# Table loads of ScalarE written out in the kernel, with Ln and Exp from one table set, in a two-layer streaming encoder

## The reference

```python
def trunk_layer(h, p_l, past_k, past_v, ...):
    mix, k, v, v_a = token_mixers(rmsnorm(h, g_mix), past_k, past_v, ...)
    h = h + mix
    h = h + peer(rmsnorm(h, g_ffn), w_peer_q, sub_keys, u_tab, v_tab)
    gate = jax.nn.sigmoid(rmsnorm(h, g_ple) @ w_ple_gate + b_ple_gate)
    h = h + (p_l @ w_ple) * gate
```

## Time and profile before

| | |
|---|---|
| timed runs, median of 3 (lowest, highest) | 3350.75 us (3350.59, 3355.32) |
| span of the profiled execution | 3616.5 us |
| ACT busy / TABLE_LOADs | 786.7 us / 313 |
| PE, DVE, POOL busy | 67%, 65%, 59% of the span |
| bytes moved, mean rate | 1277 MB, 353 GB/s |

### The profile page before, as it was taken

How to read it: one execution, slowest core, us unless ns; L and a number is a source line. 1 busy time by engine, 2 the same in 40 slices (tenths; PEclk the granted TensorE clock), 3 DMA queues, 4 the chain that set the end, 5 groups by cost and what they waited for, 6 DMA issues and landing times.

```text
span 3616.5 us, 28348 instructions
## 1 busy us (share of the span) xinstructions
PE 2438.9 (67%) x8364; PEld 999.6 (28%) x8364; DVE 2348.9 (65%) x5973; ACT 786.7 (22%) x1403; POOL 2133.1 (59%) x2201
## 2 busy tenths in 40 slices
PE   7547748989855467878554588878965455756546
PEld 4313313443411123334111124334331112211111
DVE  1576596557688876565786766555678776654552
ACT  4104112553100022231000131544200111200012
POOL 0265565556666666666666666555666666666661
PEclk9778869988866679989766799987977767887778
DMA  6599999989989999999999999998999999999993
GB/s 234 211 387 380 357 359 350 336 302 347 376 333 354 353 383 412 414 382 399 360 358 350 363 358 403 362 342 299 398 386 338 366 361 361 412 389 371 365 377 131
DMA packets 330209, 1277.02 MB, mean 353 GB/s; under 512 B 37380, under 2 KB 38404, under 8 KB 322760
## 3 DMA queue, kind: packets, MB, share of 16 engines
q0 software_dynamic: 313344, 1140.99, 83.2%
q1 hardware_dynamic: 16712, 134.21, 9.3%
HBM read 1267.45 MB, written 6.82 MB: 352 GB/s over the span
## 4 chain that ended last, share of the span: by engine, by line
PE 30%; DVE 28%; issue 15%; another core or an unknown queue 9%; POOL 7%; DMA 6%; ACT 5%; DVEq 0%; POOLq 0%; ACTq 0%; SPq 0%
DVE urows L1313 11%; PE experts L1615 9%; PE bank L1585 9%; DMA vrows<-in_peer_v,idx_v 4%; POOL urows L902 4%; POOL vrows L902 4%; PE bank L1595 3%; PE att_out L1585 2%; DVE work L1198 2%; DMA urows<-in_peer_u,idx 1%; DVE part L1274 1%; DVE work L1264 1%; DVE diag L1350 1%; DVE work L1268 1%
## 5 line engine op out<-in xcount | busy, mean ns | idle before, releaser
L1615 PE MATMUL experts<-vrows,diag 128*64 128x512 f32 (+1 forms) x3896 | 1220.7, 765 | 824.2 <-DVE diag L1350 329.3
L1313 DVE CUSTOM_DVE_ANT_0 urows<-urows,query 128x1024 f32<-128x1024 f32 x1088 | 1307.7, 1212 | 302.4 <-DMA urows<-in_peer_u,idx 202.8
L902 POOL DMA_INDIRECT urows<-in_peer_u,idx x1024 | 1005.6, 982 | 547.4 <-issue 289.9
L902 POOL DMA_INDIRECT vrows<-in_peer_v,idx_v x910 | 883.9, 971 | 719.5 <-PE experts L1615 347.1
L1615 PEld LDWEIGHTS experts<-vrows,diag 128*64 128x64 f32 (+1 forms) x3896 | 305.8, 165 | 1577.4 <-issue 1197.9
L1585 PE MATMUL bank<-weights,xT 128*128 128x512 f32 (+1 forms) x1008 | 469.7, 618 | 27.2 <-issue 20.7
L1585 PEld LDWEIGHTS bank<-weights,xT 128*128 128x128 f32 (+1 forms) x1008 | 175.8, 181 | 306.0 <-issue 295.8
L1595 PE MATMUL bank<-xT,weights 128*128 128x288 f32 (+2 forms) x688 | 152.2, 379 | 33.6 <-issue 23.4
L958 ACT ACTIVATE work<-bank 128x256 f32<-128x256 f32 (+2 forms) x67 | 29.2, 437 | 642.5 <-PE bank L1809 199.6
L902 POOL DMA_INDIRECT vrows<-in_peer_v,idx x114 | 114.6, 1005 | 75.7 <-PE experts L1615 32.4
L1361 DVE SCALAR_TENSOR_TENSOR h<-vrows,plain,h 128x1024 f32<-128x1024 f32 x114 | 146.3, 1284 | 0.0
(11 more groups left out here) (212 smaller groups left out, 2556.2 us busy)
## 6 DMA issues: line engine op xcount, KB each, us to landing
weights<-in_w_in SPq DMA_DIRECT2D x25, 2048.0 KB
weights<-in_w_out SPq DMA_DIRECT2D x10, 2048.0 KB
weights<-in_w_peer_q SPq DMA_DIRECT2D x10, 2048.0 KB
urows<-in_peer_u,idx POOLq DMA_INDIRECT x1024
weights<-in_w_ple_gate SPq DMA_DIRECT2D x8, 2048.0 KB
vrows<-in_peer_v,idx_v POOLq DMA_INDIRECT x910
weights<-in_w_ple SPq DMA_DIRECT2D x4, 1024.0 KB
weights<-in_sub_keysT SPq DMA_DIRECT2D x5, 512.0 KB
```

The lines of the kernel that those rows point to most:

```text
L902: pool.indirect_dma_start(out=rows[:, where, :], out_offset=None, in_=table, in_offset=bass.IndirectOffsetOnAxis(ap=index, axis=0))\
L1313: dve.tensor_tensor_reduce(row, row, query[:, :], 1.0, 0.0, ALU.mult, ALU.add, hid[:, j % 2, k:k + 1]).then_inc(dotted.sem, 1)
L1615: last = pe.matmul(experts[c][HALF * x:HALF * x + wide, :], diag[:, (4 * j + q) % ND, k % QUARTER + x, 0:wide], vrows[:, (n + x) % NV, 512 ...
```

## The change

ScalarE's stream asks for its sets itself. A function names the set of each stage, and behind a stage that uses one, the set of the next stage that uses a different one is asked for.

```diff
+LOG_EXP, GELU, SIGMOID = "natural_log_exp_and_others", "gelu_and_others", "sigmoid_and_others"
+
+
+def table_of(s):
+
+    k = s[0]
+    if k in ("ua", "va") or (k == "peer" and s[2] == 0 and 0 < s[1] <= ITEM_COUNT):
+        return GELU
+    if k == "gate":
+        return SIGMOID
+    if k in ("squares", "vaQ", "attQ", "mixQ", "attZ", "samZ", "attE", "samX") or (k == "choice" and s[4] == 0):
+        return LOG_EXP
+    return None
...
+            table_uses = [x for x in SCHEDULE if table_of(x)]
+
+            def next_table(s):
+
+                n = table_uses.index(s) + 1
+                if n < len(table_uses) and table_of(table_uses[n]) != table_of(s):
+                    act.preload_act_table_set(table_of(table_uses[n]))
...
+            act.preload_act_table_set(table_of(table_uses[0]))
             act.wait_ge(const_made, 1)
             for s in SCHEDULE:
...
+                if table_of(s):
+                    next_table(s)
```

## The result

The changed kernel takes **3321.55 us** (median of 4 runs, 3316.86 to 3329.72) against 3352.67 us of the kernel before, timed beside it: a ratio of 0.990, with a 95% interval of 0.9883 to 0.9916, or 31 us less. The forecast was 3309.5 us, 41.3 us less, with a range of 3268 to 3344. Direction and order of size came out; two of the three terms did not have the size that they were given, and their errors partly cancel.

What follows compares the result with a forecast made beforehand. The prediction took transfers to set the pace in most of the kernel, with ScalarE's table loads on the path at the ends and in attention. 7.7 + 5.2 + 28.4 = 41.3 us off 3350.75 gave 3309.5 us, range 3268 to 3344.

Steps and rivals of the forecast that it cites:

- The price of a load: Anywhere on the path: one table load removed from ScalarE lets the next instruction start 1.29 us earlier.
- First tile: Before any gather: six loads on the path, 1.29 us each, bring the first gather forward by 7.7 us.
- The step on the weights: First tile: the 2 MB weight unit lands at about 11 us, barely hidden before TensorE's first product at 11.35.
- Last tile: After the last gather: four loads on the path, at 1.29 us each, save 5.2 us.
- The middle: From 133 to 3547 us: 22 of 42 removed loads on the chain count, all in the attention stretches, 28.4 us.
- the room in the attention stretches: Two attention stretches at 310 and 322 GB/s: transfers could speed up to 361 GB/s, leaving room for 25 and 23 us.
- The loads elsewhere: Middle outside the attention stretches: 20 loads on the chain (25.8 us), counted at nothing because DMA is at 0.94 or above.
- The moved loads: Loads that stay but move, some passing over ScalarE's copies: taken as 0, from 15 us lost to 19 us gained.
- the slower rival: Moved loads delay copies others wait for, 29.9 us in full, and the middle gains nothing: 3368 us, chance 0.08.
- Only the ends: Rival: only first and last tile gain, 12.9 us, as the middle waits for transfers: 3338 us, chance 0.20.
- The whole chain: Rival: all 54.2 us of the middle's chain count besides the ends, 67.1 us in all: 3284 us, chance 0.16.
- the drain: Rival: each table switch costs twice its load, as a hidden drain goes too: 3268 or 3265 us, chance 0.01.

Runs made afterwards that it cites:

- half gathers: Kernel before and changed kernel, each with gathers of 512 floats per token instead of 1024: 3221.83 us with the old loads, 3174.62 us with the change.
- the kernel with the middle alone: Against the kernel before, only the stages between the first and the last gather changed (175 loads): 3337.21 us, ratio 0.9942.
- the second profile: The kernel before, unchanged, profiled once more: span 3350.4 us, timed 3355.81 us, ratio 0.9998.
- the first profile: The kernel before, as profiled for the prediction: span 3616.5 us, against timed runs with a median of 3350.75 us.

## Why the prediction was right, and where it was not

The total came out inside the range partly by luck: a first tile that was too small and a middle that was too large offset each other, and within the middle the gain was made elsewhere than forecast.

- **The price of a load, 1.29 us.** Right: Square to Exp is shorter by 2.56 us for two loads, and with half gathers ten loads at the norms gave 11.4 of 12.8 us. And the Trainium skill's 2.66 us for a switch (ScalarE: Activation LUTs, "What ACT_TABLE_LOAD costs") is not borne out here: the removed switches gave back no drain. In the trace the next ACTIVATE stands 0.01 us behind its load.
- **First tile, 7.7 us.** Too small: 12.9 and 10.4 us in the two profiles of the changed kernel, against 133.27. The step that failed is that TensorE's products behind the stalls were taken over with their old durations; seven pieces at a higher clock make 5.7 us in the first of the two. How much of that the change brings, and how much the single execution, stays open, since the kernel with the middle alone had 4.4 us of it with the old loads. The step on the weights had the right place and was off by 0.6 us: they landed at 11.84, and the product began at 11.98, not at 11.35, so that here the transfer was the one that ended the wait.
- **Last tile, 5.2 us.** Right: 5.3 and 5.1 us in the profiles.
- **The middle, 28.4 us.** Too large: 15.6 us as the mean of two profiles. The step that failed is the room in the attention stretches. It was worked out from the transfers' 310 and 322 GB/s, and TensorE, busy for 92% and 91% of the stretches in the second profile, was not counted as next late. Instead of 14 us each they are 4 us shorter or 3 longer, and 3 or 4 shorter, and with half gathers they gain nothing; the prediction's own sign of being wrong, stretches as long as before, is what came. Part of the error is the first profile: its span was 7.9% above the timed runs, and this was put to the profiler in general, not to its transfers, and handled by scaling the sum. With the second profile the same steps would have had 29 loads on the chain instead of 42, and 7 instead of 22 in the attention stretches. The loads elsewhere, counted at nothing, gave more (11 us by the time of the kernel that changes them alone) than those counted in full (4.7 us). The reason given for the nothing, transfers that set the pace, took back only a part: at the norms 7 or 8 of 11.4 us.
- **The moved loads, 0.** Right as far as it can be told, from minus to plus a few microseconds; the slower rival (29.9 us of delays on the path) did not show.
- **The rivals.** Only the ends would be 3338: the transfers took back a part of the middle and not all. The whole chain would be 3284: out, and so is the drain (3265 to 3268). The forecast gain is 10 us above the measured one: a first tile given 3 to 5 us too little offset in part a middle given 13 us too much.

## What to carry to other kernels

When functions that alternate come from two table sets, look for one set that holds both and ask for it: here this halved the loads, and where the loads then stand made no difference that could be measured. Count in full only the loads on a path with nothing beside it: next to transfers at their ceiling more than half came back as waits for data, and in stretches where TensorE was busy for over 90% they gave next to nothing. Before a term is given room, look at every engine of the stretch, and not only at the one that seems late. And before rows of a profile price anything, compare its span with the timed runs: if it is some per cent longer, find out which resource was slow in it, since its chain of waits is then not the one of the timed runs.

## What was not expected of the hardware

One execution of the kernel before moved 353 GB/s in the mean and 350 to 380 GB/s in its gather stretches, another of the same kernel 381 and about 410, and their spans are 3616.5 and 3350.4 us. TensorE's granted clock behind a stall in the first tile was 0.63 to 0.69 from 60 to 80 us in six executions with the old loads, and 0.83 and 1.00 in a seventh with the same instructions there; 16 products of 128x512 took 9.12 and 6.94 us. Half of the gathered bytes shortened the kernel by 4% only.
